# Moving the second one-hots to ScalarE and re-dealing spread chunks and fetched rows

## The chip, the cores and the metric

One core of one Trainium2 chip. The metric is device time in microseconds of one execution, the median of several runs.

## The reference, cut to what matters

A 1-layer encoder step for 1024 prompt tokens and 128 sample tokens (9 tiles of 128). Per tile: `x += W_o(sig(g_a)*SB(xn) W_oa + sig(g_b)*SWA(xn) W_ob)`, then `x += PEER(RMSNorm(x))`, then a final RMSNorm. SB is stick-breaking attention, causal, 8 heads of 64. PEER is a retrieval over 128 x 128 experts, 8 heads, the best 16 of each:

```python
q = (tb @ wq).reshape(PEER_BLOCK, PEER_HEADS, 2, PEER_HALF)
sc = jnp.einsum('thpd,pnd->thpn', q, subkeys)
sv, si = lax.top_k(sc, PEER_TOPK)
cv, ci = lax.top_k(cand, PEER_TOPK)      # cand: all sums of two halves' best
e = i1 * PEER_KEYS + i2                   # 16 experts for each head and token
g = jax.nn.softmax(cv, axis=-1)
h = jnp.einsum('thkd,td->thk', u[e], tb)
a = (jax.nn.gelu(h, approximate=False) * g)
return jnp.einsum('thk,thkd->td', a, v[e])
```

## The kernel before, in words

Four programs run one after another: project, window, sample_attention, decide, and then dense; the change is in **decide** (L885 to L1648). It walks the nine tiles in SEQUENCE (the sample tile first, then prompt tiles 0 to 7) as stages i = 0 to 8. Stage i (from 1 on) holds, on TensorE, the stick-breaking attention of its tile in i positions (`attend(t, n)`, n = 0 to i-1), the projections by w_oa and w_ob (`projected`), the router's queries of the tile before (`queries`, 16 blocks of 8 products of 128x128, four groups of four blocks), a transposition of the gated sum (`turned_sum`), the router's scores (`scores_of`) and the product with w_o (`merge`). Each engine runs a list in program order that is written out by hand; semaphores tie them.

VectorE picks experts: `residual` (y = merge + x), `halves_best` (five steps of 16 instructions for the best 16 of each half), `pairs_best`, `gated`, `experts_of` (the selection of the expert numbers: two rounds of test, product and sum over 128x2048, L1242 to L1245), `weigh` (after ScalarE's softmax). Between the steps it does two other kinds of work:

- **Fetched rows.** The sample tile's experts are fetched one row per token at a time by GpSimd's indirect DMA into a ring of RB = 4 buffers (L1128), 128 times for u (the row product with xg, L1280) and 128 times for v (acc += a * row, L1284). `fetch(n)` takes the next n of these 256. FETCH[i][n] stands beside position n, and AFTER[i] as one block at the end of the stage, between `weigh` and the next `residual`. Row 129 waits for Gelu over the 128 sums, which ScalarE makes in stage 5.
- **One-hots.** For four prompt tiles (DENSE = 4) the chosen weights are spread into a dense matrix G. 128 chunks of QUAD = 4 tokens: for each token, first (128x128, is iota equal to the first number) times second (iota equal to the second number, times the weight) by one TensorE product. VectorE makes first (L1299) and second (L1302, four instructions) in `one_hots`, DEEP = 2 buffers each; TensorE multiplies in `spread_out` (L1502) into banks 6 and 7; ScalarE copies them out in `take` (L1376), and every eighth chunk issues a 2 MB store of G.

Chunks stand at these places: WOVEN[i][n] = 4 in each position from stage 4 on (one at each of four points in `attend`; in stage 4 not in the first position), and BESIDE[i] = 4 in stages 6 to 8 between the projections and the queries. The order is the same on the three engines, so that TensorE at the start of `attend(t, 0)` needs a first and a second one-hot, which VectorE makes only after AFTER's block and `residual`. Without a chunk there (stages 2 to 4) it needs y itself before the first product of the values (L1551). `normed` (L1178, L1182) waits for ScalarE's sum of squares, which ScalarE makes between the first and the second position. ScalarE copies the scores out (L1432) only when VectorE has finished its second sum (`sum2`), since the two share a buffer.

```python
def spread_out(n):
    for c in range(written[0], written[0] + n):
        pe.wait_ge(onehots, c + 1)
        if c >= 2:
            pe.wait_ge(taken, c - 1)
```

The end of the stages: `residual(8)`, `normed(8)`, `halves_best(7)`, `pairs_best(7)`, `experts_of(7)`, then the same for tile 8; beside it TensorE's last `queries` and `scores_of`. The next program, dense, starts when all engines are done.

Of the kernel before, what the change touches and what calls it, by code (L numbers as in the profile page):

```python
# [5 lines left out]
BF16 = mybir.dt.bfloat16  # L6
I32 = mybir.dt.int32
# [6 lines left out]
P = 128  # L14
# [870 lines left out]
def decide(nc, a, o):  # L885
# [13 lines left out]
    LOW = -3e38  # L899
    dense = lambda i: 1 <= i <= DENSE  # L900
# [9 lines left out]
    with ExitStack() as ctx:  # L910
# [7 lines left out]
        mask_f = sb("c_mask_f", [P, P])  # L918
        ident_b, mask_b = sb("c_ident_b", [P, P], BF16), sb("c_mask_b", [P, 4, P], BF16)
        zero_b = sb("c_zero_b", [P, 512], BF16)  # L920
# [15 lines left out]
        top, top_i, top_f = sb("c_top", [P, 16, 16]), sb("c_topi", [P, 16, 16], U32), sb("c_topf", [P, 16, 17])  # L936
        cv, ci = sb("c_cv", [P, 8, 16]), sb("c_ci", [P, 8, 16], U32)
        parts_i = sb("c_partsi", [P, 3, 8, 16], U32)
# [3 lines left out]
        expert, idx_new = sb("c_expert", [P, P]), sb("c_idxn", [P, P], I32)  # L942
        row_f, row_u, row_v = sb("c_rowf", [P, P]), sb("c_rowu", [P, P], I32), sb("c_rowv", [P, P], I32)
        iota = sb("c_iota", [P, P])
        turned = sb("c_turned", [P, DENSE, 3, P])
        first = [sb(f"c_first{n}", [P, QUAD, P]) for n in range(DEEP)]
        second = [sb(f"c_second{n}", [P, QUAD, P]) for n in range(DEEP)]
        spread = [sb(f"c_spread{u}", [P, P, TS]) for u in range(2)]
        gw, gw_first, h_sb, aw = sb("c_g", [P, P]), sb("c_gfirst", [P, P]), sb("c_h", [P, P]), sb("c_a", [P, P])
        small = sb("c_small", [P, 4])  # L950
# [14 lines left out]
        onehots, spread_done, taken = sem("c_onehots"), sem("c_spread_done"), sem("c_taken")  # L965
# [13 lines left out]
                      "topf low mid high col mid2 high2 rest place rise hot1 pick1 sum1 hot2 pick2 sum2 expert index")  # L979
# [6 lines left out]
        flat = lambda x: x.rearrange("p c q -> p (c q)")  # L986

        with nc.Block() as block:
            @block.sync
            def _(sp):  # L990
                for dst, src in ((ident[:], a["ident"]), (negtri[:], a["negtri"]), (mask_f[:], a["mask"])):
                    sp.dma_start(dst, src).then_inc(tabs, 16)
# [139 lines left out]
            def _(dve):  # L1132
# [81 lines left out]
                def pairs_best(j):  # L1214
                    halves = top[:].rearrange("p (h s) k -> p h s k", s=2)
# [14 lines left out]
                def experts_of(j):  # L1230
# [60 lines left out]
                def one_hots(n, beside=0):  # L1291

                    for c in range(made[0], made[0] + n):
                        q, tok = c * QUAD // P, c * QUAD % P
                        if tok == 0:
                            dve.wait_ge(turned_done, q + 1)
# [736 lines left out]
```

## Time and profile before

| | us |
|---|---|
| median of 3 runs | 4262.68 (4256.29 to 4276.88) |
| profiled execution | 4258.31 |
| its span | 4256.5 |
| mean granted TensorE clock | 0.921 |
| TensorE busy | 3628.3 (85%) |
| VectorE busy | 2795.3 (66%) |
| ScalarE busy | 912.5 (21%) |
| GpSimd busy | 1004.9 (24%) |

decide lies between about 842 and 2357 us of the span. The stages are most easily told by ScalarE's copy of the attention's sum (oaT, L1459), one in each: 972.4, 1054.9, 1181.7, 1328.2, 1504.6, 1705.8, 1926.4 and 2150.8 us for stages 1 to 8. "Granted clock" is the TensorE clock that the throttle allowed, as a share of full speed. In a row of the timeline the first number is the start, the second the time from the first to the last instruction of a merged group, and the bracket holds the engine's idle time before it and what ended that.

### The profile page before, as it was taken

To read this page: it belongs to the slowest core of one execution; us is meant where nothing else is said; L and a number is where in the kernel's file an instruction comes from. 1 tells how busy PE (TensorE), PEld (TensorE's weight loads), DVE (VectorE), ACT (ScalarE), POOL (GpSimd) and SP (SyncE) were. 2 spreads that over 40 slices of the span, in tenths; PEclk is the share of its full clock that TensorE was granted. 3 is DMA by queue.
4 is the path that set the end of the run, shared out by engine and by line. 5 is a ranking of instruction groups with operands and counts; after the bars stand their busy time and mean duration, and the time that the engine had idled before them with its cause. 6 is when DMAs were issued, how large, how long until landed. Compare 5 with 4: busy or idle time off the path is not lost. (4 is left out here: it accounts for less than half of the span.)

```text
span 4256.5 us, 47064 instructions
## 1 busy us (share of the span) xinstructions
PE 3628.3 (85%) x15116; PEld 2211.3 (52%) x15116; DVE 2795.3 (66%) x5522; ACT 912.5 (21%) x1696; POOL 1004.9 (24%) x862
## 2 busy tenths in 40 slices
PE   7999868977879677687883499999999998999998
PEld 5999854443657456465663144444434443444443
DVE  4111063417577667666768498888878887888876
ACT  1111154512224426162621000010000000010001
POOL 0000000002331221302120243333334333333331
PEclk9999987988999788888896699999999999999999
DMA  2222327866987675757574899999999999999994
GB/s 101 84 85 84 108 60 293 350 229 215 328 272 243 205 242 172 251 182 243 182 244 136 329 392 410 403 399 402 384 384 390 365 390 382 362 399 401 391 377 198
DMA packets 334914, 1178.00 MB, mean 277 GB/s; under 512 B 28584, under 2 KB 145496, under 8 KB 256408
## 3 DMA queue, kind: packets, MB, share of 16 engines
q0 software_dynamic: 113280, 680.84, 41.4%
q1 hardware_dynamic: 219168, 461.71, 31.0%
q10 hardware_dynamic: 2304, 33.56, 1.9%
q8 instruction: 70, 1.15, 0.1%
q14 instruction: 92, 0.75, 0.1%
HBM read 1104.56 MB, written 72.48 MB: 277 GB/s over the span
## 5 line engine op out<-in xcount | busy, mean ns | idle before, releaser
L1919 PE MATMUL d_ps<-d_xd,d_u 128*128 128x512 f32 x2048 | 917.9, 602 | 137.9 <-DMA d_u<-u_blocks 126.0
L1930 PE MATMUL d_ps<-d_v,d_a 128*128 128x512 f32 x2048 | 904.7, 595 | 28.6 <-DVE d_a L1822 22.2
L1762 POOL DMA_INDIRECT d_ring<-peer_uv,d_idx x512 | 654.8, 1279 | 1118.2 <-DVEq L1815 1015.2
L1919 PEld LDWEIGHTS d_ps<-d_xd,d_u 128*128 128x128 f32 x2048 | 394.9, 193 | 641.0 <-issue 623.0
L1813 DVE SCALAR_TENSOR_TENSOR d_acc<-d_ring,d_aw,d_acc 128x1024 f32<-128x1024 f32 x512 | 657.7, 1285 | 101.8 <-DVE d_acc L1813 65.3
L1801 DVE SCALAR_TENSOR_TENSOR d_ring<-d_ring,d_xn 128x1024 f32<-128x1024 f32 x512 | 605.0, 1220 | 88.9 <-DMA d_qacc<-ys 52.5
L1930 PEld LDWEIGHTS d_ps<-d_v,d_a 128*128 128x128 f32 x2048 | 390.1, 191 | 524.4 <-issue 524.3
L1128 POOL DMA_INDIRECT c_ring<-peer_uv,c_rowu x128 | 149.2, 1166 | 756.9 <-DVE c_ring L1280 381.7
L1502 PE MATMUL c_ps<-c_second,c_first 128*128 128x128 f32 x1024 | 147.8, 292 | 195.9 <-DVE c_second L1302 195.9
L1884 ACT ACTIVATE d_ge<-d_h (+1 forms) x256 | 52.0, 203 | 1144.6 <-DVE d_ring L1801 1144.5
L1128 POOL DMA_INDIRECT c_ring<-peer_uv,c_rowv x128 | 162.6, 1270 | 529.2 <-DVEq L1286 509.0
L1603 PE MATMUL c_ps<-c_mT,c_chunk 128*128 128x128 f32 x2304 | 269.1, 280 | 15.7 <-DMA c_chunk<-wq 13.5
L1603 PEld LDWEIGHTS c_ps<-c_mT,c_chunk 128*128 128x128 f32 x2304 | 265.7, 196 | 21.4 <-DMA c_chunk<-wq 10.2
L1502 PEld LDWEIGHTS c_ps<-c_second,c_first 128*128 128x128 f32 x1024 | 136.1, 202 | 237.5 <-DVE c_second L1302 202.4
L164 DVE CAST a_w_high<-a_w 128x2048 fp32r<-128x2048 f32 x17 | 20.9, 1227 | 343.6 <-DMA a_w<-w_in 343.6
L257 PE MATMUL a_ps<-a_w_low,a_x_high 128*128 128x256 f32 (+1 forms) x792 | 220.6, 279 | 4.6 <-ACT a_stage L214 4.6
L1280 DVE SCALAR_TENSOR_TENSOR c_ring<-c_ring,c_xg 128x1024 f32<-128x1024 f32 x128 | 155.7, 1226 | 99.6 <-DMA c_ring<-peer_uv,c_rowu 99.1
L257 PE MATMUL a_ps<-a_w_high,a_x_high 128*128 128x256 f32 (+1 forms) x792 | 219.9, 278 | 0.0
L257 PE MATMUL a_ps<-a_w_high,a_x_low 128*128 128x256 f32 (+1 forms) x792 | 219.6, 277 | 0.0
L1829 DVE TENSOR_TENSOR d_qacc<-d_ps,d_qacc 128x512 f32<-128x512 f32 x256 | 169.6, 685 | 69.4 <-PE d_ps L1930 69.4
L1284 DVE SCALAR_TENSOR_TENSOR c_acc<-c_ring,c_a,c_acc 128x1024 f32<-128x1024 f32 x128 | 164.3, 1284 | 66.6 <-DMA c_ring<-peer_uv,c_rowv 58.1
L1511 PE MATMUL c_ps<-c_q,c_k 64*128 64x128 f32 (+1 forms) x1152 | 165.3, 298 | 0.7 <-ACT c_sc L1432 0.7
(274 smaller groups left out, 4559.8 us busy)
## 6 DMA issues: line engine op xcount, KB each, us to landing
c_chunk<-wq SPq DMA_DIRECT2D x144, 512.0 KB, 4.9
d_u<-u_blocks SPq DMA_DIRECT2D x128, 512.0 KB, 18.1
d_v<-v_blocks SPq DMA_DIRECT2D x128, 512.0 KB, 16.4
s_kc<-sb_kT SPq DMA_DIRECT2D x32, 1024.0 KB, 8.7
s_vc<-sb_v SPq DMA_DIRECT2D x32, 1024.0 KB, 7.0
G<-c_spread ACTq DMA_DIRECT2D x16, 2048.0 KB, 9.7
d_gb<-G SPq DMA_DIRECT2D x32, 1024.0 KB, 42.7
c_chunk<-w_oa SPq DMA_DIRECT2D x36, 512.0 KB, 6.8
```

The lines of the kernel that those rows point to most:

```text
L257: last = nc.tensor.matmul(out, lhsT(left, k), rhs(right, k), start=(k == 0 and n == 0), stop=(k == KC - 1 and n == 2))
L1128: pool.indirect_dma_start(out=ring[:, k % RB], out_offset=None, in_=rows, in_offset=bass.IndirectOffsetOnAxis(ap=source[:, k % P:k % P + 1 ...
L1284: nc.vector.scalar_tensor_tensor(acc[:], ring[:, r], aw[:, s:s + 1], acc[:], ALU.mult, ALU.add).then_inc(summed, 1)
L1502: last = nc.tensor.matmul(ps[:, SPREAD + c % 2, k * P:(k + 1) * P], first[c % DEEP][:, k], second[c % DEEP][:, k], start=True, stop=True)
L1511: last = nc.tensor.matmul(ps[:, bank + par, c * P:(c + 1) * P], k_sb[p % 2][0:rows, x], q_sb[0:rows, x], start=(c == 0 or n > 0 and stop), ...
L1603: last = nc.tensor.matmul(ps[:, w // 4, (w % 4) * P:(w % 4 + 1) * P], wq[:, c * P:(c + 1) * P], xT[:, c], start=(c == 0), stop=(c == KC - 1))
L1762: pool.indirect_dma_start(out=ring[:, b], out_offset=None, in_=a["peer_uv"], in_offset=bass.IndirectOffsetOnAxis(ap=idx8[par][:, b:b + 1], ...
L1801: last = nc.vector.scalar_tensor_tensor(ring[:, b, 0:D], ring[:, b, 0:D], 1.0, xn[T % 2][:], ALU.mult, ALU.mult, accum_out=h[:, bass.ds(co ...
L1813: nc.vector.scalar_tensor_tensor(acc[T % 2][:], ring[:, b, D:], aw[:, bass.ds(col + n, 1)], acc[T % 2][:], ALU.mult, ALU.add).then_inc(sum ...
L1829: nc.vector.tensor_tensor(part, ps[:, VB + c % 4, :], part, ALU.add).then_inc(v_taken, 1)
L1919: last = nc.tensor.matmul(ps[:, HB + x % 2, :], ub[j][:, k], xd[:, k].rearrange("p t q -> p (t q)"), start=(k == 0), stop=(k == KC - 1))
L1930: last = nc.tensor.matmul(ps[:, VB + c % 4, :], A[u][j][:, q * P:(q + 1) * P], vb[u][j][:, half * 512:half * 512 + 512], start=(j == 0), s ...
```

## The change

- The second one-hots are made by ScalarE (`second_halves`): four Abs of iota minus the number (a pointer as bias), then, in place, four Relu of weight minus weight times that distance (pointers as bias and scale). `turned` therefore holds four tables instead of three (number, minus number, minus weight, weight), and ScalarE copies them in three instructions. VectorE keeps the first one-hots (`first_halves`), with FIRSTS = 3 buffers.
- WOVEN: one chunk per position instead of four. SLOTS: 18 chunks a stage from stage 4 on in the products of projections, queries, scores and merge (2 + 2, then 1 and 2 in turn behind every second block of the queries, 1, 1). The nine that are left stand behind the last queries.
- FETCH: three rows per position from stage 5 on, LOOKUPS: one row before each of the six big steps of `experts_of`, from stage 3 on; AFTER is shorter; six rows are left for the end.
- Small ones: the small instructions of `experts_of` in another order and one less in parts_i, several buffers shared to make room, and the opening and closing product of the sum's bank takes a 128-column zero as weights.

```diff
-    WOVEN = [[0] * i for i in range(4)] + [[0, 4, 4, 4]] + [[4] * i for i in range(5, NT)]
-    BESIDE = [0, 0, 0, 0, 0, 0, 4, 4, 4]
-    FETCH = [[], [0], [12, 16], [0, 4, 6], [0, 0, 3, 4]] + [[0] * 5 + [3] * (i - 5) for i in range(5, NT)]
-    AFTER = [0, 8, 18, 26, 25, 31, 31, 27, 27]
+    WOVEN = [[1 if i > DENSE or i == DENSE and n else 0 for n in range(i)] for i in range(NT)]
+    SLOTS = [18 if i >= DENSE else 0 for i in range(NT)]
+    FETCH = [[], [0], [7, 7], [0, 0, 0], [2, 2, 2, 2]] + [[3] * i for i in range(5, NT)]
+    LOOKUPS = [0, 0, 0] + [6] * (NT - 3)
+    AFTER = [0, 6, 22, 14, 14, 18, 16, 14, 10]
+    FIRSTS = 3
...
# VectorE
-                        for k in range(QUAD):
-                            last = nc.vector.tensor_scalar(second[c % DEEP][:, k], iota[:], turned[:, q, 1, tok + k:tok + k + 1],
-                                                           turned[:, q, 2, tok + k:tok + k + 1], ALU.is_equal, ALU.mult)
-                        last.then_inc(onehots, 1)
...
+                def lookups_of(i, n):
+
+                    if SLOTS[i]:
+                        first_halves(3 if n > 3 else 2)
+                    fetch(LOOKUPS[i] // 6)
...
                     pairs_best(i - 2)
-                    one_hots(BESIDE[i])
+                    if SLOTS[i]:
+                        first_halves(4)
                     gated(i)
-                    experts_of(i - 2)
+                    experts_of(i - 2, lambda n: lookups_of(i, n))
...
                 pairs_best(NT - 2)
+                first_halves(P - made[0])
                 experts_of(NT - 2)
                 weigh(NT - 2)
+                fetch(2 * P - fetches[0])
...
# ScalarE
+                        if c >= DEEP:
+                            act.wait_ge(spread_done, c - DEEP + 1)
+                        for k in range(QUAD):
+                            nc.scalar.activation(second[c % DEEP][:, k], iota[:], ACT.Abs, bias=turned[:, q, 1, tok + k:tok + k + 1]).then_inc(away, 1)
+                        act.wait_ge(away, QUAD * (c + 1))
+                        for k in range(QUAD):
+                            last = nc.scalar.activation(second[c % DEEP][:, k], second[c % DEEP][:, k], ACT.Relu,
+                                                        bias=turned[:, q, 3, tok + k:tok + k + 1], scale=turned[:, q, 2, tok + k:tok + k + 1])
+                        last.then_inc(second_done, 1)
...
+                def spread_one(on):
+
+                    if on and evicted[0] < P:
+                        take(1)
+                        second_halves(evicted[0] + DEEP - seconds[0])
...
                     for g in range(4):
                         act.wait_ge(eaten, ROUTE_AT[j] + 4 * (g + 1))
                         nc.scalar.activation(flat(qT[:, 4 * g:4 * g + 4]), ps[:, g, :], ACT.Copy).then_inc(act_r.sem, 1)
+                        for n in range(3):
+                            spread_one(slots)
...
+                        if i == 4:
+                            second_halves(DEEP)
...
                         moved_x(i - 1)
-                        take(BESIDE[i])
-                        queries(i - 1)
+                        for n in range(4):
+                            spread_one(SLOTS[i])
+                        queries(i - 1, SLOTS[i])
...
-                queries(NT - 1)
+                queries(NT - 1, 0)
+                for n in range(P - evicted[0]):
+                    spread_one(True)
...
# TensorE
-                        pe.wait_ge(onehots, c + 1)
+                        pe.wait_ge(first_done, c + 1)
+                        pe.wait_ge(second_done, c + 1)
...
                         last.then_inc(eaten, 1)
+                        if w % 2:
+                            spread_out(slots * (w % 4 // 2 + 1))
...
                     turned_sum(i)
                     if i > 1:
                         scores_of(i - 1)
+                    spread_out(1 if SLOTS[i] else 0)
                     merge(i)
+                    spread_out(1 if SLOTS[i] else 0)
```

## Rows read from the trace of the kernel before

**Rows 1.** Waits between 850 and 2360 us: total, times, longest.

```profile
PE c_ps L1502 <- DVE c_second L1302: 195.9, 28, 43.3
```

**Rows 2.** Window of stage 6: length; busy PE, PEld, DVE, ACT, POOL; clock; DMA.

```profile
1505.00:1706.00 201.00, 148.07 (x905) 113.44 (x905) 136.49 (x404) 82.32 (x118) 43.16 (x34) 0.86 0.65 217
```

**Rows 3.** TensorE's timeline, the long stops behind stages 3 to 7.

```profile
1275.46 0.58 PE L1551 MATMUL c_ps<-c_zero_b,c_ident_b 128*128 128x512 bf16 x1 [21.13 <-DVE c_y L1171]
...
1422.95 2.08 PE L1502 MATMUL c_ps<-c_second,c_first 128*128 128x128 f32 x8 [30.53 <-DVE c_second L1302]
...
1612.20 2.08 PE L1502 MATMUL c_ps<-c_second,c_first 128*128 128x128 f32 x8 [43.30 <-DVE c_second L1302]
...
1818.26 2.08 PE L1502 MATMUL c_ps<-c_second,c_first 128*128 128x128 f32 x8 [42.73 <-DVE c_second L1302]
...
2031.34 2.08 PE L1502 MATMUL c_ps<-c_second,c_first 128*128 128x128 f32 x8 [35.14 <-DVE c_second L1302]
```

**Rows 4.** VectorE's timeline, the end of stage 6: weigh, first and last row, residual.

```profile
1755.40 0.29 DVE L1259 TENSOR_REDUCE c_gsum<-c_g 128x8 f32<-128x128 f32 x1 [10.48 <-ACT c_g L1410]
...
1756.17 1.28 DVE L1284 SCALAR_TENSOR_TENSOR c_acc<-c_ring,c_a,c_acc 128x1024 f32<-128x1024 f32 x1
...
1813.86 1.28 DVE L1284 SCALAR_TENSOR_TENSOR c_acc<-c_ring,c_a,c_acc 128x1024 f32<-128x1024 f32 x1 [0.55 <-DMA c_ring<-peer_uv,c_rowv]
1815.36 1.23 DVE L1171 TENSOR_TENSOR c_y<-c_ps,c_y 128x1024 f32<-128x1024 f32 x1 [0.21 <-DVE c_acc L1284]
```

**Rows 5.** Groups by line and shape, ScalarE's narrow instructions: busy us, mean ns.

```profile
L1410 ACT ACTIVATE c_g<-c_g 128x128 f32<-128x128 f32 x9 | 2.7, 304 | 37.1 <-DVE c_g L1228 37.1
...
L214 ACT ACTIVATE a_stage<-a_ps 128x256 f32<-128x256 f32 x90 | 34.6, 384 | 217.2 <-PE a_ps L257 217.2
L486 ACT ACTIVATE b_S<-b_S,b_neg 128x256 f32<-128x256 f32 x64 | 31.5, 495 | 31.0 <-DVE b_ds L433 31.0
```

**Rows 6.** ScalarE's timeline, positions of stage 7.

```profile
1852.35 1.14 ACT L1396 ACTIVATE c_soft<-c_soft 128x512 f32<-128x512 f32 x2
...
1856.95 0.60 ACT L1403 ACTIVATE c_soft<-c_ps 128x512 f32<-128x512 f32 x1 [0.26 <-PE c_ps L1546]
...
1921.38 0.60 ACT L1403 ACTIVATE c_soft<-c_ps 128x512 f32<-128x512 f32 x1 [0.18 <-PE c_ps L1546]
...
1926.37 0.60 ACT L1459 ACTIVATE c_oaT<-c_ps 128x512 f32<-128x512 f32 x1 [0.43 <-ACT c_spread L1376]
```

**Rows 7.** Stage 6, oaT copy to the end of merge: ScalarE's rows, then TensorE's.

```profile
1705.81 0.60 ACT L1459 ACTIVATE c_oaT<-c_ps 128x512 f32<-128x512 f32 x1 [0.43 <-ACT c_spread L1376]
...
1755.07 0.30 ACT L1410 ACTIVATE c_g<-c_g 128x128 f32<-128x128 f32 x1
...
1720.30 1.95 PE L1502 MATMUL c_ps<-c_second,c_first 128*128 128x128 f32 x16
...
1725.79 28.75 PE L1603 MATMUL c_ps<-c_mT,c_chunk 128*128 128x128 f32 x256
...
1758.82 13.90 PE L1586 MATMUL c_ps<-c_wo,c_mT 128*128 128x512 f32 x32
```

**Rows 8.** VectorE's timeline behind the last stage: residual, then experts_of.

```profile
2252.59 1.23 DVE L1171 TENSOR_TENSOR c_y<-c_ps,c_y 128x1024 f32<-128x1024 f32 x1 [0.21 <-DVE c_acc L1284]
...
2287.97 0.29 DVE L1231 CAST c_topf<-c_topi 128x256 f32<-128x256 uint32 x1
```

**Rows 9.** Clock after stops: TensorE's timeline, windows; the page's group of wq.

```profile
1157.61 3.78 PE L1540 MATMUL c_ps<-c_soft,c_negtri 128*128 128x512 f32 x4 [3.13 <-ACT c_soft L1390]
3656.24 7.13 PE L1930 MATMUL d_ps<-d_v,d_a 128*128 128x512 f32 x16 [2.60 <-DVE d_a L1822]
...
1157.00:1162.00 5.00, 4.39 (x7) 0.50 1.03 371
1162.00:1171.00 9.00, 9.00 (x35) 0.53 0.80 264
...
L1603 PE MATMUL c_ps<-c_mT,c_chunk 128*128 128x128 f32 x2304 | 269.1, 280 | 15.7 <-DMA c_chunk<-wq 13.5
```

More of the change, by code:

```diff
@@ L941, in decide @@
         choice = sb("c_choice", [P, 2, 8, 16])
-        expert, idx_new = sb("c_expert", [P, P]), sb("c_idxn", [P, P], I32)
-        row_f, row_u, row_v = sb("c_rowf", [P, P]), sb("c_rowu", [P, P], I32), sb("c_rowv", [P, P], I32)
+        idx_new = sb("c_idxn", [P, P], I32)
+        expert = flat(part[:, 0])
+        row_u, row_v = sb("c_rowu", [P, P], I32), sb("c_rowv", [P, P], I32)
         iota = sb("c_iota", [P, P])
-        turned = sb("c_turned", [P, DENSE, 3, P])
-        first = [sb(f"c_first{n}", [P, QUAD, P]) for n in range(DEEP)]
+        turned = sb("c_turned", [P, DENSE, 4, P])
+        first = [sb(f"c_first{n}", [P, QUAD, P]) for n in range(FIRSTS)]
+        mask_f = first[0][:, 0]
         second = [sb(f"c_second{n}", [P, QUAD, P]) for n in range(DEEP)]
@@ L1443, in _ @@
                 moved_x(0)
-                queries(0)
+                queries(0, 0)
                 scores_of(0)
@@ L1468, in _ @@
                         scores_of(i - 1)
+                        for n in range(2):
+                            spread_one(SLOTS[i])
                     if i == GELU_AT:
@@ L1501, in spread_out @@
                         for k in range(QUAD):
-                            last = nc.tensor.matmul(ps[:, SPREAD + c % 2, k * P:(k + 1) * P], first[c % DEEP][:, k], second[c % DEEP][:, k], start=True, stop=True)
+                            last = nc.tensor.matmul(ps[:, SPREAD + c % 2, k * P:(k + 1) * P], first[c % FIRSTS][:, k], second[c % DEEP][:, k], start=True, stop=True)
                         last.then_inc(spread_done, 1)
@@ L1550, in attend @@
                         pe.wait_ge(dve_m.sem, dve_m.at(t, "y"))
-                        nc.tensor.matmul(ps[:, SUM, :], ident_b[:], zero_b[:], start=True, stop=False)
+                        nc.tensor.matmul(ps[:, SUM, :], zero_b[:], flat(mask_b[:]), start=True, stop=False)
                     for par in range(2):
@@ L1619, in _ @@
                 turned_x(0)
-                queries(0)
+                queries(0, 0)
                 scores_of(0)
@@ L1630, in _ @@
                     for n in range(1, t + 1):
-                        attend(t, n, WOVEN[i][n] // 4)
-                    nc.tensor.matmul(ps[:, SUM, :], ident_b[:], zero_b[:], start=False, stop=True).then_inc(pe_m.sem, 1)
+                        attend(t, n, WOVEN[i][n])
+                    nc.tensor.matmul(ps[:, SUM, :], zero_b[:], flat(mask_b[:]), start=False, stop=True).then_inc(pe_m.sem, 1)
                     if i > 1:
@@ L1637, in _ @@
                     if i > 1:
-                        spread_out(BESIDE[i])
-                        queries(i - 1)
+                        queries(i - 1, 1 if SLOTS[i] else 0)
                     turned_sum(i)
```

103 lines of the change are left out of this document (56 added, 47 removed).

## The prediction

> **What bounds the kernel now.** I read the waits first: in the third program (decide) TensorE waits longest for VectorE's second one-hots, 195.9 us in 28 waits, the longest 43.3 [rows 1]. Then a stage, from one oaT copy to the next: in the 201 us of stage 6 TensorE is busy 148 and VectorE 136 [rows 2], so no sum of busy times decides; what is late at the hand-over does. TensorE's timeline shows it: one long stop a stage, of 21.1, 30.5, 43.3, 42.7 and 35.1 us behind stages 3 to 7, always for something that VectorE makes in or after residual [rows 3]. VectorE's timeline shows what it does meanwhile: at the end of stage 6 it starts the 31 fetched rows of AFTER at 1756.17, ends with row 31 at 1813.86 and only then adds the residual [rows 4]. That is 59.2 us for 31 rows, 1.91 us each, against 1.50 from start to start where rows lie ready: row transfers set that pace. So the stop is the fetch block, less what TensorE still had to do.
>
> **Part 1, fewer rows in the block.** AFTER goes from 26, 25, 31, 31, 27, 27 to 14, 14, 18, 16, 14, 10 in stages 3 to 8. The 59.2 us split into four rows that waited in the ring, at 1.50, and 27 at 1.97; so 14 rows take 25.7 us, 16 take 29.6, 18 take 33.6 and 10 take 17.8 (bounds: 1.50 and 2.2 each). The rows return as three per position (4.5 us beside a position of 12.9), six between the selection steps, where VectorE was idle 10.5 us for the softmax [rows 4], and six at the end. Stage 3 has no spread chunks yet, so there it is a plain gain: VectorE is done at about 1252, TensorE needs y at 1254.3, and the stop of 21.1 goes, with 1.3 us of slow clock behind it: **-22 us**. In stages 1 and 2 twelve rows less are fetched while the DMA engines are full; worth between 0 and -8, taken as 0, since the rows still queue behind each other.
>
> **Part 2, the second one-hots on ScalarE.** Per chunk VectorE loses four instructions of 346 ns (1.0 us with overlap) and ScalarE gains eight of 128x128. A narrow one without a pointer takes 304 ns [rows 5]; a bias pointer makes 128x256 take 495 where 384 stands without [rows 5], so about 0.10 more; two in a row overlap by 0.10 (1.14 us for two of 0.62 [rows 6]). Abs with a bias pointer: 0.30 a step. Relu has a scale pointer too, which no row shows: 0.30 if it is free, 0.40 if it costs what the bias does. I take 0.40: 4 x 0.30 + 0.10 for the wait + 4 x 0.40 = **2.9 us** a chunk, 2.5 if free, 3.6 with no overlap at all, 1.7 if pointers cost nothing in a row of eight.
> The Trainium skill (ScalarE: Activation LUTs, the section on what ACT_TABLE_LOAD costs) says that every per-partition pointer operand adds about 93 ns and that neighbours overlap by about as much; by it the chunk costs 2.8 us, which speaks against the change, where by the plain narrow row it would be 1.7 and the change clearly faster.
>
> **Part 3, the positions.** A position of stage 7 takes 12.89 us on average, from its last exp (L1403) at 1856.95 to that of the position five later at 1921.38 [rows 6], with four chunk copies of 0.9 to 1.1 in it. One copy and one second half replace four copies. Chain after: values and one chunk 2.35, scores 2.0, back row 1.03, copy 0.87, second half 2.9, exps 1.04, to the last exp 2.7 = 12.9. **No gain per position.** At the first position three copies, their waits and one DMA issue go (-6.7), 2.9 and 0.5 for two more copies of turned come, and VectorE's second one-hots (1.0) go: -4.3. The next one gains nothing and loses 2.0, since the copies stood beside VectorE's wait; behind the last exp oaT comes 2.0 instead of 5.0 us later: -3.0. Together -5.3 a stage, **-21 us** for stages 5 to 8. In stage 4 ScalarE makes two second halves (5.8) ahead of rms, which holds back normed and the first chunk: **+4 us**.
>
> **Part 4, the products of merge and router.** Now 18 chunks a stage stand here, where 0 (stages 4 and 5) or 4 stood. I count from the start of the oaT copy. Projections with four chunks: to 18.4 (14.5 to the end of the products, four chunks at 0.97 [rows 7]). Then the queries, four groups of 7.2 us, with one chunk behind the second block and two behind the fourth. ScalarE waits for the fourth block before it copies anything, and the third chunk's second half can only be made after chunk one is copied: qT 0.5, copy 0.87, second half 2.9, so TensorE stands **3.3 us in every group**. A group takes 7.2 + 1.0 + 4.3 + 1.0 = 13.5; ScalarE's own work in it, 11.7, still fits. The fourth group's products end at 67; ScalarE then has three copies and three second halves before softmax (78.8) and mT; merge ends at 94, where it ended at 66.9 in stage 6 (1705.81 to 1772.7 [rows 7]). Softmax was at 49.3 [rows 7]. VectorE weighs until 80.1 and starts its block, then residual and one first one-hot, 2.15. TensorE goes on at 108 in stage 4 (before 94.8), 115.6 in stage 5 (107.6; 17 rows, Gelu, one row), 111.9 in stage 6 (112.5), 108 in stage 7 (104.9), and residual stands at 98.1 in stage 8 (101.8). Sum **+20 us**. VectorE's first one-hots don't set it: the last of the stage waits for the first chunk behind the fourth group, so selection ends near 73.
>
> **Part 5, the end.** WOVEN and SLOTS place 29 + 90 = 119 chunks; nine are left, and six rows. Behind the last residual VectorE needs 35.4 us to experts_of (2252.59 to 2287.97 [rows 8]). Now it makes nine first one-hots there; the ninth waits for chunk six, and ScalarE makes a chunk in 3.75 us, beginning with the last qT copy at 40.4: 40.4 + 4 x 3.75 + 1.05 + 0.7 = 57. That is +21.7, the six rows +9.9, and 1.5 of an old wait go: **+30 us**, bounds +22 and +34.
>
> **Part 6, the clock.** After a stop TensorE often runs at the lower of its levels (1.2 GHz of 2.4): after one of 3.13 us the granted clock was 0.50 for 5 us and 0.53 for 9 more, 6.3 us lost; after the long ones the first chunk takes 2.08 instead of 1.05; yet after one of 2.60 us the products ran at full pace [rows 9]. The 20 new stops are of 3.3 us, nearest the first of these. Each that falls costs about 2.0 us (as behind the long stops), at least 0, at most 6.3. I take half of them: **+20 us**, between 0 and +40.
>
> **Sum** against the profiled execution (span 4256.5, with what lies around it 4258.3): -22 - 21 + 4 + 20 + 30 = +11, with the clock +31: 4289. The median of the runs, 4262.7, is 4.4 higher, less than they differ among themselves, so I forecast 4289. Some 63 second halves lie on the path (31 in positions, 28 before softmax, 4 at the end): each 0.1 us of them moves the sum by 6 us.
>
> **Rivals.**
> (a) The clock holds at the 20 stops, as behind the 2.60 us one: 4269. Chance 0.25, no measurable change.
> (b) Faster: the eight narrow instructions go at 0.20 a step, as rows without a pointer would give, so a chunk costs 1.7. Positions fall to 11.7, the stop in a group to 2.1, where the clock would mostly hold: 4269 - 63 x 1.2 = 4193. For it: 304 ns is a real row, and Abs and Relu need no table. Against it: the 495 ns row. It decides from 2.4 us a chunk down (then 4238). Chance 0.2, with rows landing faster than 1.9 us counted in.
> (c) The clock falls at each stop as at 1157: 20 x 6.3 on 4269 = 4395. That stop lay beside full DMA queues and three more ScalarE waits; chance 0.07.
> (d) The queries' weight chunks come late, now that rows are fetched beside them: as in stage 2, where nearly all of the 13.5 us fell that TensorE waited for wq [rows 9], the longest 4.82; five stages, 67 us on the forecast, 4356. Against it: a group now takes 13.5 us for the same 2 MB. Chance 0.05.
>
> **Numbers.** Forecast case 0.43, within it 4265 to 4325. The range reaches down over (a) and part of (b), up to a second half of 3.3 us with the clock falling at most stops: 4218 to 4345. What this kernel's measurement can tell from no change is about 0.5%, 21 us: faster 0.22 (b and the low end of a), same 0.31 (a, and the part of the forecast case under 4284), slower 0.47.
>
> **What would show it.** Right: ScalarE's Abs near 0.39 us and Relu near 0.48; in the queries TensorE idle four times a stage for some 3 us, released by ScalarE's second; the long stops down to 15 to 25 us with TensorE's merge ending at 94; positions still near 12.9; the stop at 1275 gone; 20 us between the last residual's selection and experts_of. Wrong: chunks in the queries without a stop, or positions under 12 us (then Part 2 fails, and it is b); a granted clock of 1.00 through the queries (a); rows in the block at 1.5 us.

## The result, and the profile after

The change makes the kernel slower: 4361.29 us (median, 4357.32 to 4380.86) against 4269.78 for the kernel before, timed beside it (4256.29 to 4284.34). The ratio is 1.0223, with a 95% interval of 1.0174 to 1.0271. The forecast was 4289, with a range of 4218 to 4345: the direction was right, and the size was too small, so that the time lies 16 us above the range. The profiled execution has a span of 4361.4 us and a granted clock of 0.915 (0.921 before).

The page's groups of the product, of the first one-hots and of ScalarE's Relu:

```profile
L1548 PE MATMUL c_ps<-c_second,c_first 128*128 128x128 f32 x1024 | 163.1, 312 | 167.5 <-DVE c_first L1308 87.1
L1308 DVE TENSOR_TENSOR c_first<-c_iota,c_turned 128x512 f32<-128x512 f32 x128 | 86.8, 691 | 281.1 <-PE c_ps L1548 280.1
L1394 ACT ACTIVATE c_second<-c_second,c_turned 128x128 f32<-128x128 f32 x512 | 211.0, 482 | 4.3
```

TensorE's waits between 850 and 2460 us (total, times, longest), where [rows 1] had one line with 195.9 us:

```profile
PE c_ps L1548 <- DVE c_first L1308: 87.1, 14, 18.4
PE c_ps L1591 <- ACT c_soft L1436: 84.7, 31, 4.7
PE c_ps L1548 <- ACT c_second L1394: 76.9, 21, 4.2
```

The wait for VectorE is less than half of what it was, and two waits for ScalarE stand beside it: the one for the second one-hots in the queries (L1394), which was forecast, and one in the positions (L1436, the logarithm that the second product of a position reads), which was not.

The window of stage 6, from one oaT copy to the next, answers to [rows 2] (length; busy PE, PEld, DVE, ACT, POOL; clock; DMA):

```profile
1724.60:1955.80 231.20, 176.47 (x969) 131.03 (x971) 122.33 (x291) 157.14 (x331) 63.33 (x43) 0.86 0.63 209
```

ScalarE went from 82 to 157 us, VectorE from 136 to 122, the stage from 201 to 231. No engine is full, as before.

**Where the time went.** I cut decide at ScalarE's oaT copies and where TensorE goes on behind residual; the last row runs from the last residual to the first instruction of dense.

| stretch | forecast | measured |
|---|---|---|
| up to the oaT copy of stage 3 | 0 | -15.8 (1181.7 to 1165.9) |
| from there to the oaT copy of stage 4 | -22 + 4 | -11.1 (146.5 to 135.4) |
| hand-overs of stages 4 to 8: oaT to TensorE going on (8: to residual) | +20, clock +20 | +46.3 |
| positions behind them, stages 5 to 8 | -21 | +33.7 |
| the end | +30 | +38.0 (104.9 to 142.8) |
| sum | +31 | +91.1 |

The positions account for 55 of the 60 us that are missing. (Of the other rows, the early gain and the end's and stage 4's shortfall nearly cancel.) Dense took 1912.8 us instead of 1899.0 with the same code. Over the kernels of this study it takes 1898.7 and 1899.0 with the old tables of rows and 1906 to 1922 in the eight kernels with the new ones, so these 14 us, which the forecast did not have, may belong to the new tables; no run shows how. For mechanisms I use the stretch **from the oaT copy of stage 3 to dense**: 1175.8 us before, 1282.7 after. It is read from one profiled execution of each kernel, and executions of one kernel differ by some 10 to 40 us, so a few us in it say nothing by themselves.

**The positions.** ScalarE's timeline through one position of stage 6:

```profile
1692.40 0.60 ACT L1439 ACTIVATE c_soft<-c_ps 128x512 f32<-128x512 f32 x1 [0.85 <-PE c_ps L1591]
...
1697.05 1.01 ACT L1429 ACTIVATE c_q<-c_ps 1x1024 f32<-1x1024 f32 x1 [0.93 <-PE c_ps L1557]
1698.09 1.06 ACT L1407 ACTIVATE c_spread<-c_ps 128x512 f32<-128x512 f32 x1
1698.96 1.23 ACT L1391 ACTIVATE c_second<-c_iota,c_turned 128x128 f32<-128x128 f32 x4
1700.22 1.65 ACT L1394 ACTIVATE c_second<-c_second,c_turned 128x128 f32<-128x128 f32 x4
1701.78 1.13 ACT L1433 ACTIVATE c_soft<-c_soft 128x512 f32<-128x512 f32 x2
1702.81 1.13 ACT L1436 ACTIVATE c_soft<-c_soft 128x512 f32<-128x512 f32 x2
1705.59 0.60 ACT L1439 ACTIVATE c_soft<-c_ps 128x512 f32<-128x512 f32 x1 [1.65 <-PE c_ps L1591]
1707.30 0.60 ACT L1439 ACTIVATE c_soft<-c_ps 128x512 f32<-128x512 f32 x1 [1.11 <-PE c_ps L1591]
```

TensorE's timeline of the same position (in the trace each f32 product of the source is two instructions; when I count products behind a stop, I count these rows):

```profile
1698.66 2.05 PE L1557 MATMUL c_ps<-c_q,c_k 64*128 64x128 f32 x16
1703.48 3.78 PE L1591 MATMUL c_ps<-c_soft,c_negtri 128*128 128x512 f32 x4 [2.76 <-ACT c_soft L1436]
1707.19 2.44 PE L1600 MATMUL c_ps<-c_soft,c_v 128*64 128x128 f32 x16
```

From 1698.96 to 1701.78 ScalarE makes the second half: 2.82 us, where 2.9 was forecast. From the last exp at 1692.40 to the first Exp (L1433) at 1701.78 are 9.4 us, where the forecast chain has 9.15. But TensorE stops meanwhile for 2.76 us, and behind the stop the four products take 3.78 us, where the same four take 1.98 at full pace (stage 4's first position, at 1238.28, ahead of any second half). It is the lower level of the clock. From the first logarithm (L1436) to the last exp it is 4.49 us here, where the forecast chain has 2.7. So positions are 15.4 us apart (1676.43 to 1722.49 for three) instead of 12.9. Between 1290 and 2240 us the waits count 26 stops at this place, 76.1 us in all: in every position but the first of a stage they are 2.2 to 4.8 us long, and the four products behind them take 3.3 to 3.8 us (once 2.5); in the first position they are 0.7 to 1.6.

**The queries.** TensorE's timeline in stage 6, one stop for each group (the third, 3.48 at 1785.79, left out), and the stop at the hand-over:

```profile
1755.59 1.13 PE L1548 MATMUL c_ps<-c_second,c_first 128*128 128x128 f32 x8 [3.51 <-ACT c_second L1394]
1770.76 2.04 PE L1548 MATMUL c_ps<-c_second,c_first 128*128 128x128 f32 x8 [3.48 <-ACT c_second L1394]
...
1800.01 1.13 PE L1548 MATMUL c_ps<-c_second,c_first 128*128 128x128 f32 x8 [4.15 <-ACT c_second L1394]
...
1839.59 2.08 PE L1548 MATMUL c_ps<-c_second,c_first 128*128 128x128 f32 x8 [13.50 <-DVE c_first L1308]
```

The stop was forecast at 3.3 us; fifteen of the 20 are 3.48 to 3.51 and five, where ScalarE also issues a store of G, 4.15 to 4.23. The first chunk behind it goes at the lower clock in 11 of 20 (1.5 to 2.05 us for 1.13), but a chunk at full pace does not mean that the clock held. In stage 6 the chunks at 1755.59 and 1785.79 both take 1.13; TensorE's two blocks behind each:

```profile
1756.56 5.36 PE L1649 MATMUL c_ps<-c_mT,c_chunk 128*128 128x128 f32 x32
...
1786.76 3.74 PE L1649 MATMUL c_ps<-c_mT,c_chunk 128*128 128x128 f32 x32
```

The chunk and the two blocks, 40 products from start to start, take 4.5 us in four of the 20 cases and 5.9 to 7.5 in the other sixteen: 29 us lost over the five stages. Softmax stands 82.5 to 86.3 us behind oaT (forecast 78.8), and the long stop is down from 42.7 to 13.5. VectorE's block of 16 rows, in that stage, starts at 1808.23 and ends with residual at 1837.71: 29.5 us, forecast 29.6.

**Stage 3.** VectorE's timeline behind the shorter block, then TensorE's:

```profile
1238.16 1.22 DVE L1176 TENSOR_TENSOR c_y<-c_ps,c_y 128x1024 f32<-128x1024 f32 x1
...
1251.79 0.16 DVE L1183 RECIPROCAL c_small<-c_small 128x1 f32<-128x1 f32 x1 [7.01 <-ACT c_small L1451]
...
1253.19 0.68 DVE L1308 TENSOR_TENSOR c_first<-c_iota,c_turned 128x512 f32<-128x512 f32 x1
```

```profile
1253.93 2.08 PE L1548 MATMUL c_ps<-c_second,c_first 128*128 128x128 f32 x8 [11.41 <-DVE c_first L1308]
```

Residual is in time, and the stop of 21.1 us [rows 3] is gone. But ScalarE makes two second halves (1243.31 to 1249.02) ahead of its sum of squares, `normed` waits for that, the first one-hot waits behind `normed`, and TensorE stops one position later for 11.4.

**The end.** VectorE's timeline:

```profile
2305.75 1.23 DVE L1176 TENSOR_TENSOR c_y<-c_ps,c_y 128x1024 f32<-128x1024 f32 x1 [0.21 <-DVE c_acc L1293]
...
2364.32 0.69 DVE L1308 TENSOR_TENSOR c_first<-c_iota,c_turned 128x512 f32<-128x512 f32 x1 [2.95 <-PE c_ps L1548]
2367.97 0.69 DVE L1308 TENSOR_TENSOR c_first<-c_iota,c_turned 128x512 f32<-128x512 f32 x1 [2.95 <-PE c_ps L1548]
2368.57 0.29 DVE L1236 CAST c_top<-c_topi 128x256 f32<-128x256 uint32 x1
...
2386.22 1.28 DVE L1293 SCALAR_TENSOR_TENSOR c_acc<-c_ring,c_a,c_acc 128x1024 f32<-128x1024 f32 x1 [0.15 <-issue]
...
2397.44 2.81 DVE L1194 MAX8 c_top<-c_sc 128x8 f32<-128x128 f32 x14 [0.35 <-DVE c_acc L1293]
```

From residual to the selection are 62.8 us (forecast 57, before 35.4), the chunks in between 3.65 us apart; the six rows take 11.2 us (forecast 9.9).

### The profile page after: what moved, and what is told of

Same layout as the page of the kernel before. It is cut to its first block and busy times, and to the rows that moved or that the text cites. A ratio compares the mean times of both kernels' runs of the same rounds, so it can differ in the third digit from the quotient of the medians.

```text
span 4361.4 us, 47602 instructions
## 1 busy us (share of the span) xinstructions
PE 3722.5 (85%) x15092; PEld 2270.4 (52%) x15116; DVE 2661.8 (61%) x5010; ACT 1258.2 (29%) x2728; POOL 1046.5 (24%) x862
## 5 line engine op out<-in xcount | busy, mean ns | idle before, releaser
L1979 PE MATMUL d_ps<-d_v,d_a 128*128 128x512 f32 x2048 | 906.7, 596 | 32.7 <-DVE d_a L1871 26.2
L1133 POOL DMA_INDIRECT c_ring<-peer_uv,c_rowu x128 | 165.5, 1293 | 791.5 <-DVE c_ring L1289 405.3
L1133 POOL DMA_INDIRECT c_ring<-peer_uv,c_rowv x128 | 187.3, 1464 | 592.4 <-DVEq L1295 566.4
L1548 PE MATMUL c_ps<-c_second,c_first 128*128 128x128 f32 x1024 | 163.1, 312 | 167.5 <-DVE c_first L1308 87.1
L1649 PE MATMUL c_ps<-c_mT,c_chunk 128*128 128x128 f32 x2304 | 287.4, 288 | 10.0 <-DMA c_chunk<-wq 7.4
L1649 PEld LDWEIGHTS c_ps<-c_mT,c_chunk 128*128 128x128 f32 x2304 | 283.0, 205 | 13.6 <-DMA c_chunk<-wq 7.3
L1308 DVE TENSOR_TENSOR c_first<-c_iota,c_turned 128x512 f32<-128x512 f32 x128 | 86.8, 691 | 281.1 <-PE c_ps L1548 280.1
L1548 PEld LDWEIGHTS c_ps<-c_second,c_first 128*128 128x128 f32 x1024 | 146.0, 220 | 186.4 <-DVE c_first L1308 96.2
L164 DVE CAST a_w_high<-a_w 128x2048 fp32r<-128x2048 f32 x17 | 20.9, 1227 | 349.8 <-DMA a_w<-w_in 349.8
L1394 ACT ACTIVATE c_second<-c_second,c_turned 128x128 f32<-128x128 f32 x512 | 211.0, 482 | 4.3
```

The lines of the kernel that those rows point to most:

```text
L1133: pool.indirect_dma_start(out=ring[:, k % RB], out_offset=None, in_=rows, in_offset=bass.IndirectOffsetOnAxis(ap=source[:, k % P:k % P + 1 ...
L1394: last = nc.scalar.activation(second[c % DEEP][:, k], second[c % DEEP][:, k], ACT.Relu, bias=turned[:, q, 3, tok + k:tok + k + 1], scale=t ...
L1548: last = nc.tensor.matmul(ps[:, SPREAD + c % 2, k * P:(k + 1) * P], first[c % FIRSTS][:, k], second[c % DEEP][:, k], start=True, stop=True)
L1649: last = nc.tensor.matmul(ps[:, w // 4, (w % 4) * P:(w % 4 + 1) * P], wq[:, c * P:(c + 1) * P], xT[:, c], start=(c == 0), stop=(c == KC - 1))
L1979: last = nc.tensor.matmul(ps[:, VB + c % 4, :], A[u][j][:, q * P:(q + 1) * P], vb[u][j][:, half * 512:half * 512 + 512], start=(j == 0), s ...
```

## The experiments

The theory after the result, A in most of the expectations: what costs is the place of the second halves on ScalarE's queue. Ahead of the exponentials and ahead of the next chunk they stop TensorE each time, and the clock adds to that.

Four kernels first, each the changed kernel with one edit.

**The second half behind the logarithms.**

```diff
-                    spread_one(woven > 0)
+                    if woven > 0:
+                        take(1)
...
                         nc.scalar.activation(soft[:, par, 1], soft[:, par, 1], ACT.Ln, bias=1.0).then_inc(act_a.sem, 1)
+                    if woven > 0:
+                        second_halves(evicted[0] + DEEP - seconds[0])
```

> The changed kernel, with one move: in each position ScalarE makes the second half of the one-hots behind the two Ln instead of ahead of the Exp. Same instructions, same counts. Theory A (the second half of 2.82 us ahead of Exp stops TensorE for 2.75 us in every position, and the clock falls to its lower level behind each such stop): both go, the position falls from 15.4 us to 11.8, over 26 positions about 85 us, so about 4276. Theory B (only the ScalarE chain is longer, the clock costs nothing): a position gains what the second half then hides beside TensorE's product, 1.65 us, about 40 us, so about 4320. Theory C (positions are not what makes the change slow; the queries and the end are): within 10 us of 4361.

Measured: 4295.67 us, ratio 1.0096 [1.0068 to 1.0123], midway between theory A (4276) and theory B (4320); from the oaT copy of stage 3 to dense 1233.2, so 49.5 less than in the changed kernel. TensorE's timeline in stage 8:

```profile
2064.41 2.47 PE L1603 MATMUL c_ps<-c_soft,c_v 128*64 128x128 f32 x16 [1.96 <-ACT c_soft L1442]
2066.81 1.82 PE L1551 MATMUL c_ps<-c_second,c_first 128*128 128x128 f32 x8
...
2074.08 1.98 PE L1594 MATMUL c_ps<-c_soft,c_negtri 128*128 128x512 f32 x4
```

The products behind the logarithm are back at 1.98 us (two last positions excepted, with 2.6); a shorter stop, 1.96, has moved to the values, and behind it these take from 1.55 us (at full pace) to 2.75. From a stage's second position on the positions are 12.0 to 14.2 us apart, 13.6 in most of stage 8. The positions of stages 5 to 8 take 388.9 us, 47.6 less than in the changed kernel (436.5), and that is nearly the whole gain of the stretch. 388.9 is also 13.9 less than before the change (402.8), where the forecast had 21 less: the place of the second half explains the positions' loss but for some 7 us.

**A chunk ahead of the qT copy in the queries.**

```diff
                     for g in range(4):
+                        spread_one(slots)
                         act.wait_ge(eaten, ROUTE_AT[j] + 4 * (g + 1))
                         nc.scalar.activation(flat(qT[:, 4 * g:4 * g + 4]), ps[:, g, :], ACT.Copy).then_inc(act_r.sem, 1)
-                        for n in range(3):
+                        for n in range(2):
                             spread_one(slots)
```

> The changed kernel, with one move: in each group of the queries ScalarE takes the first of the three chunks (copy and second half) before it waits for the fourth block, not behind it. Theory A (the 20 stops of 3.5 us in the queries come from this order, and softmax, the rows behind it and residual all follow): the stops shrink below 1.6 us, since ScalarE's 11.7 us of work in a group of 10.2 then sets the pace; softmax comes at about 68 us behind the oaT copy instead of 84; 15 us in each of five stages, about 4286. Theory B (softmax comes earlier, but VectorE's selection with its rows and first one-hots is then the late one): at most 5 us a stage, about 4336.

Measured: 4297.96, ratio 1.0099 [1.0072 to 1.0125], nearer to theory A (4286); the stretch 1228.8, so 53.9 less. TensorE's timeline, the queries of one stage:

```profile
1948.60 1.13 PE L1549 MATMUL c_ps<-c_second,c_first 128*128 128x128 f32 x8 [1.81 <-issue]
1949.56 3.74 PE L1650 MATMUL c_ps<-c_mT,c_chunk 128*128 128x128 f32 x32
...
1960.12 1.13 PE L1549 MATMUL c_ps<-c_second,c_first 128*128 128x128 f32 x8 [1.46 <-DVE c_first L1308]
1961.09 3.74 PE L1650 MATMUL c_ps<-c_mT,c_chunk 128*128 128x128 f32 x32
```

The stops are 1.1 to 2.1 us (one is below 0.5), and the 40 products behind them are within 0.3 us of full pace but for two cases, both behind a stop of 2.08. Softmax comes at 72.1 instead of some 84 us behind oaT, in every stage, and the hand-overs of stages 4 to 8 are 58.7 us shorter (509.3 for 568.0); the other stretches give 4.8 back. The twenty stops sum to 32 us where they were 73, and the clock's loss behind them to 4 where it was 29. Now ScalarE has no idle time in a group: 11.5 us from one to the next (1948.60 to 1960.12) are its own work.

**Products that fill TensorE's stop.** Twelve products of 128x512 with a zero matrix as weights, into a bank whose content isn't used then, from the third position of a stage on: two positions of stage 4 and 18 of the 26 in stages 5 to 8. They change no result.

```diff
+                    if woven > 0 and n > 1:
+                        for f in range(FILL):
+                            nc.tensor.matmul(ps[:, TURN, :], zero_b[:], flat(mask_b[:]), start=True, stop=True)
```

> The changed kernel, with 12 small bf16 products into an unused bank on TensorE ahead of its wait for Ln, in positions from the third on (20 positions); nothing reads them. They only keep TensorE busy where it stood for 2.75 us. Theory A (the clock falls behind that stop): the products of Ln and of the values run at full pace, a position falls from 15.4 to about 13 us, 20 positions, some 45 us, so about 4316. Theory B (the clock is not it, the chain is): no change or slightly slower, 4361 to 4375.

Measured: 4322.95, ratio 1.0165 [1.0125 to 1.0206], near theory A (4316); the interval overlaps that of the changed kernel (1.0174 to 1.0271), so the trace has to carry the reading. The stretch is 1255.5, so 27.2 less. TensorE's timeline:

```profile
1881.59 2.76 PE L1592 MATMUL c_ps<-c_mask_b,c_zero_b 128*128 128x512 bf16 x12
1885.09 1.98 PE L1595 MATMUL c_ps<-c_soft,c_negtri 128*128 128x512 f32 x4 [0.74 <-ACT c_soft L1437]
1887.00 1.84 PE L1604 MATMUL c_ps<-c_soft,c_v 128*64 128x128 f32 x16
```

ScalarE's work and its order are as in the changed kernel, and the needed products start no sooner behind the scores (5.49 us from start to start, 4.82 there); only TensorE is busy meanwhile. The four products go back from 3.78 to 1.98 us and the values from 2.44 to 1.84. From a stage's second position on the positions are mostly 13.1 to 14.6 us apart, where those of the changed kernel are 14.5 to 16.1. Two of them wait 3.2 and 4.8 us for the DMA of k, a wait that the changed kernel does not have there, and take 17.6 and 20.9. With these two the positions of stages 5 to 8 take 419.0 us, 17.5 less; the rest of the 27.2 lies in the hand-overs (6.0), at the end (1.9) and in stage 4 (1.8), and I can't tell it from the scatter. So part of the positions' loss is the clock alone: in the changed kernel the four products and the sixteen of the values behind such a stop take 5.6 us on average, from start to start, and 3.7 in this row. Useless work shortened the stretch.

**The end: first one-hots between the steps of halves_best.** The nine first one-hots are dealt out between VectorE's steps of the last `halves_best`, and TensorE and ScalarE take the nine chunks inside the last queries.

```diff
-                halves_best(NT - 2)
+                halves_best(NT - 2, lambda n: first_halves(1 if n == 4 else 2))
                 pairs_best(NT - 2)
-                first_halves(P - made[0])
...
-                queries(NT - 1, 0)
-                spread_out(P - written[0])
+                queries(NT - 1, 1)
```

> The changed kernel, with the last nine chunks moved from behind the last queries into them (TensorE and ScalarE as in the other stages), and VectorE's nine first one-hots between the steps of the selection before. Theory A (the nine chunks in a row, 3.65 us each, hold the last selections up): VectorE reaches the expert numbers of tile 7 about 20 us sooner, about 4340. Theory B (VectorE then waits just as long inside the selection): within 5 us of 4361.

Measured: 4355.95, ratio 1.0234 [1.0202 to 1.0266]. From the last residual to the selection 58.8 us instead of 62.8, to dense 138.5 instead of 142.8; the stretch 1283.2, not less. Theory B held: VectorE waits for the same chunks, only now inside the selection. Moving a wait doesn't shorten it while ScalarE's queue behind it has the same length.

Then four kernels that combine, or take the parts of the change alone.

**Three moves together.** The first two edits above, and at the end both the nine first one-hots and the six rows between the last selection's big steps (`experts_of`).

```diff
-                first_halves(P - made[0])
-                experts_of(NT - 2)
+
+                def last_lookups(n):
+                    first_halves(2 if n < 3 else 1)
+                    fetch(1)
+
+                experts_of(NT - 2, last_lookups)
```

> The changed kernel with three moves of order: the second half behind Ln in the positions, the first chunk of a group before the qT copy, and at the end VectorE's nine first one-hots and the six rows dealt out between its last selection steps instead of ahead of them and behind. If the stops are independent (theory A) the gains add: 54 + 52 and about 15 for the end on 4350, about 4230 where before stands at 4255, so slightly faster than before. If another wait takes over (theory B, for example the row blocks setting the pace), less than 90 in all, 4265 or more.

Measured: 4224.75, ratio 0.992 [0.9894 to 0.9946]; the stretch 1152.2, so 130.5 less than in the changed kernel. The end is 130.8 (142.8). The moves add up (49.5 + 53.9 + 12 = 115) and a little more, as theory A said. The same instructions in another order are worth 3% of the kernel, and turn slower into slightly faster.

**The kernel before, with the new tables of rows alone.** One-hots, chunks and queues stay as before; FETCH, LOOKUPS and AFTER are those of the change.

```diff
-    FETCH = [[], [0], [12, 16], [0, 4, 6], [0, 0, 3, 4]] + [[0] * 5 + [3] * (i - 5) for i in range(5, NT)]
-    AFTER = [0, 8, 18, 26, 25, 31, 31, 27, 27]
+    FETCH = [[], [0], [7, 7], [0, 0, 0], [2, 2, 2, 2]] + [[3] * i for i in range(5, NT)]
+    LOOKUPS = [0, 0, 0] + [6] * (NT - 3)
+    AFTER = [0, 6, 22, 14, 14, 18, 16, 14, 10]
...
-                    experts_of(i - 2)
+                    experts_of(i - 2, lambda n: fetch(LOOKUPS[i] // 6))
...
+                fetch(2 * P - fetches[0])
```

> The kernel before with the new tables of rows alone (three per position, six between the selection steps, the short blocks, six rows at the end); one-hots and chunks stay as before. Theory A (the long stops are the row blocks, and shortening them is the good part of the change): the stop at the end of stage 3 goes (-21), those of 4 to 7 and the wait of 8 shrink by 21 to 33 us each, VectorE gets late in the positions by about 2.4 us each in 20 of them (+48) and the six rows cost 10: about 4255 - 90 = 4165. Theory B (VectorE, with 6.6 us of one-hots and 4.5 of rows in a position, sets the pace there and eats all of it): 4240 to 4270.

Measured: **4132.2 us, ratio 0.9713** [0.966 to 0.9767], the fastest kernel here, faster than both and than theory A (4165); the stretch 1068.2 against 1175.8. TensorE's timeline (the first row's window ends after five of the eight products), the long stops that answer to 43.3 and 42.7 us in [rows 3]:

```profile
1531.78 1.43 PE L1507 MATMUL c_ps<-c_second,c_first 128*128 128x128 f32 x5 [18.14 <-DVE c_second L1306]
```

```profile
1715.17 2.08 PE L1507 MATMUL c_ps<-c_second,c_first 128*128 128x128 f32 x8 [13.07 <-DVE c_second L1306]
```

This is Part 1 of the forecast by itself. TensorE goes on 20.2, 22.4, 27.9 and 20.9 us earlier behind oaT in stages 4 to 7 (74.6, 85.2, 84.6 and 84.1), and the positions of stages 5 to 8 take 18.2 us more (421.0 against 402.8); there TensorE now stops up to 2.39 us for a second one-hot, behind VectorE's rows.

**The changed kernel, with the old tables of rows.**

```diff
-    FETCH = [[], [0], [7, 7], [0, 0, 0], [2, 2, 2, 2]] + [[3] * i for i in range(5, NT)]
-    LOOKUPS = [0, 0, 0] + [6] * (NT - 3)
-    AFTER = [0, 6, 22, 14, 14, 18, 16, 14, 10]
+    FETCH = [[], [0], [12, 16], [0, 4, 6], [0, 0, 3, 4]] + [[0] * 5 + [3] * (i - 5) for i in range(5, NT)]
+    LOOKUPS = [0] * NT
+    AFTER = [0, 8, 18, 26, 25, 31, 31, 27, 27]
```

> The changed kernel with the old tables of rows (long blocks at the ends of the stages, none between the selection steps). Theory A (re-dealing gains by itself some 20 to 30 us a stage also with the chunks in their new places): about 4350 + 145 = 4495. Theory B (the blocks were hidden behind the late softmax and merge anyway): within 40 us of 4350.

Measured: 4524.22, ratio 1.0624 [1.0591 to 1.0656], as theory A said (4495); the stretch 1437.5, so 154.8 more. The positions take as long as in the changed kernel (440.0 us against 436.5 in stages 5 to 8): the three rows that stand in each of them cost nothing there, and aren't what made them slow. ScalarE's oaT copy of stage 3:

```profile
1181.55 0.60 ACT L1500 ACTIVATE c_oaT<-c_ps 128x512 f32<-128x512 f32 x1 [0.46 <-remote]
```

That is the time of the kernel before (1181.7). The eight kernels with the new tables, the changed one among them, reach it between 1151.5 and 1166 us. Counted from stage 1's oaT copy, which leaves the earlier programs out, it is 209.2 and 209.4 us with the old tables and 182 to 193 with the new. So the rows that are gone from there are worth 17 to 27 us: twelve in stages 1 and 2, and ten in the positions of stage 3.

**The changed kernel, with the second one-hots back on VectorE.** ScalarE only copies; the chunks stay where the change put them.

```diff
# VectorE, behind each first one-hot
+                        if c >= DEEP:
+                            dve.wait_ge(spread_done, c - DEEP + 1)
+                        for k in range(QUAD):
+                            last = nc.vector.tensor_scalar(second[c % DEEP][:, k], iota[:], turned[:, q, 1, tok + k:tok + k + 1],
+                                                           turned[:, q, 2, tok + k:tok + k + 1], ALU.is_equal, ALU.mult)
+                        last.then_inc(first_done, 1)
# ScalarE
                         take(1)
-                        second_halves(evicted[0] + DEEP - seconds[0])
```

> The changed kernel with the second one-hots still made by VectorE (four instructions behind each first one-hot, from a table without the minus signs), everything else as changed: chunks, rows, buffers. Theory A (it is ScalarE's 2.82 us a chunk that costs, both in the positions and in the groups): positions fall to about 11 us, the stops in the groups to below 1 us, softmax to about 68; VectorE's share in the queries grows to about 50 us, its last pick near 72; about 4350 - 26 x 4 - 5 x 12 = 4185. Theory B (the places of the chunks are what costs, whoever makes the one-hots): 4320 to 4350.

Measured: 4167.47, ratio 0.9779 [0.9728 to 0.983], as theory A said (4185); the stretch 1100.9, so **181.8 less** than in the changed kernel. By stretches: stage 3 -16.8, hand-overs of stages 4 to 8 -74.7, positions of stages 5 to 8 -82.1 (354.4 against 436.5; before 402.8), the end -8.2. Inside the queries TensorE's stops are down to 0.8 to 1.4 us. What is left is the stop at the hand-over and one in the first position, both for VectorE, as in stage 6:

```profile
1747.42 2.08 PE L1550 MATMUL c_ps<-c_second,c_first 128*128 128x128 f32 x8 [15.53 <-DVE c_second L1313]
1769.94 2.07 PE L1550 MATMUL c_ps<-c_second,c_first 128*128 128x128 f32 x8 [6.60 <-DVE c_second L1313]
```

From a stage's second position on most positions are 10.2 to 11.0 us apart; four times TensorE now waits for the DMA of k, 14.8 us in all.

**The parts of the change, set out.** Dealing the rows out is worth -107.6 us behind stage 3 in the old frame and -154.8 in the new one. Moving chunks into the queries, with the second one-hots still VectorE's, costs 1100.9 - 1068.2 = +32.7: the positions gain 66.6, the hand-overs lose 95.0, stage 4 gains 11 and the end loses 15. (This is one profile against another; the intervals of the two ratios, 0.966 to 0.9767 and 0.9728 to 0.983, overlap.) Giving the second one-hots to ScalarE costs +181.8. Together -107.6 + 32.7 + 181.8 = +106.9, which is 1282.7 - 1175.8. Of the 181.8 a better order gives back 130.5; with the three moves the kernel is still 51.3 us behind the one that leaves the second one-hots on VectorE (1152.2 against 1100.9). The change holds one part worth 3% and another that costs 4%, and the second hid the first.

## Why the forecast was right and wrong

**Part 1, the block: right in the stages it worked out.** 16 rows took 29.5 us (29.6 forecast). Two of its terms were off. What comes before stage 3's oaT copy, "taken as 0" with a bound of -8 for twelve rows, is worth 17 to 27 us, and there the forecast left out that the positions of stage 3 have ten rows less too; two profiles at 1181.6 and eight at or below 1166 leave no doubt about the sign. And stage 3's gain of 22 was given back in part by the two second halves ahead of rms: priced at 4, they and the wait behind them left 11.1 of 18.

**Part 2, the instructions: right.** 2.82 us a chunk for 2.9. Over the stages Abs took 387 ns and Relu 482: the scale pointer costs what the bias does. The Trainium skill (ScalarE: Activation LUTs, what ACT_TABLE_LOAD costs) says about 93 ns for each pointer operand; the trace agrees, with 95 ns between 387 and 482. Rival b, with 1.7 us a chunk, was wrong.

**Part 3, the positions: the step that failed.** "No gain per position" rested on a chain at full clock: "exps 1.04, to the last exp 2.7 = 12.9". Its terms up to the Exp hold (9.4 for 9.15). The term "to the last exp 2.7" does not: it measured 4.49, and 2.69 where the filler kept TensorE busy (1884.42 to 1887.11 there). What the chain lacked is that TensorE stands idle for 2.76 us in it, and that the products behind run at the lower clock. Its own arithmetic showed the stop: 2.9 us of second half between the scores and the exps is 2.9 us without work for TensorE. Part 6 then gave a clock cost to the "20 new stops" of the queries only; those of the positions, one in each but the first of a stage, just as new and nearly as long, stand nowhere. With them the positions were 33.7 us longer where 21 less was forecast. The runs put it so: 47.6 us of the positions come back with the second half behind the logarithms, and 17.5 with nothing but TensorE kept busy.

**Part 4, the queries: right.** The stops are 3.48 us and more for 3.3. TensorE went on at 113.2, 121.0, 115.0 and 115.6 us behind oaT in stages 4 to 7, and residual stood at 103.2 in stage 8; forecast without clock 108, 115.6, 111.9, 108 and 98.1. That is +46.3 for the +20 and the +20 of Part 6. Softmax came 28 us later than 78.8, summed over the five stages, about the 29 us that the clock took there; without them some +17 stand against the +20 of this part. The kernel with the chunk ahead of the copy returned 58.7 in the hand-overs, so that whole loss was a matter of order.

**Part 5, the end: the right terms, mis-sized.** 27.4 us for 21.7 in front of the selection, 11.2 for 9.9 of rows; +38.0 lies 4 us outside its bounds. The last qT copy, forecast at 40.4 us behind residual, comes at 43.8 (2349.51), and of the chunks behind it, 3.65 us apart for 3.75, one takes 5.7; these two terms are nearly all of the 5.7 us that were missing.

**Part 6, the clock: too low where it was applied, and wrong in its count.** It fell behind sixteen of the 20 stops and not behind half of them, for 1.4 to 2.9 us each, 29 us in all for the +20: inside its bounds of 0 and +40. That the stops of the positions have no term at all is told above. The rivals a, c and d didn't come: the clock did not hold, it fell for single groups of products and not for 14 us, and TensorE waited less for wq, 7.4 us on the page, than before [rows 9].

What stays open: no kernel filled the stops of the queries, so their 29 us of clock are read from the changed kernel's own trace and not from an experiment. Why four equal stops left TensorE at full pace is not known. And how the gain ahead of stage 3's oaT copy splits between the stages wasn't taken apart.

## What to carry to other kernels

Work given to an idle engine costs what stands behind it on that engine's queue: ask for each piece whose next instruction another engine waits for, and put the piece behind that one. Count every stop that a chain holds for TensorE, also in the stretches that come out even, and give each the clock's price, not only those that are new to the list. When a change has several parts, time each alone: here one of them was the best version, and another hid it. And keep both questions apart, where on a queue a piece of work stands and whether it should be on that engine at all: here the order was worth 130 us and the engine another 51.

## What the runs showed of the hardware that was not expected

- Stops of 2.7 to 2.8 us in a loop of 15 us bring TensorE to its lower level (1.2 GHz of 2.4) in every turn: four products 3.3 to 3.8 us for 1.98. Stops of 1.4 to 1.8 us in the queries with the chunk ahead of the copy don't (1.13 us for the chunk behind, the blocks at 3.74 for two), and neither does one of 0.74. Equal stops of 1.96 left the values at anything from 1.55 to 2.75.
- Length alone doesn't decide. Before, a stop of 2.60 us had left the products behind it at full pace [rows 9]. In the changed kernel a stop of 1.41 us in the first position of stage 8 was followed by four products of 3.44 us, and at the end of decide six chunks in a row, each behind a stop of 1.6 us, took 2.05 for 1.13.
- Of 20 stops of 3.5 to 4.2 us in the queries, 16 cost 1.4 to 2.9 us in the 40 products behind them and four cost nothing. In five of the 16 the first eight products were still at full pace and the slow ones came after, so the first group behind a stop doesn't show what the stop cost.
- Twelve useless products in each of 20 positions made the stretch 27 us shorter.
